# A four-layer decoder step on one core: page numbers batch by batch, weight splits behind ScalarE's copies, two output slots begun with six heads

## The reference, cut to what matters

```python
q, k, v, gate = split(x @ in_w, 4)
# prompt: causal
p = softmax(where(mask, q_c . k_c / 8, -inf)); w = p[:, :, 0] - lam * p[:, :, 1]; o = w @ v
# sample: k_past = cache_k[page_table], v_past = cache_v[page_table]
p = softmax(concat(q . k_past, causal(q . k_new))); w = p[:, :, 0] - lam * p[:, :, 1]
o = w[..., :n_past] @ v_past + w[..., n_past:] @ v
o = rms_norm(o, subln_w) * (1 - lam_init)
mixer = (o * silu(gate)) @ out_w
x = layer_norm(alpha * x + mixer)
```

## Time and profile before

| | |
|---|---|
| median of 3 runs | 1701.72 us |
| lowest, highest | 1694.31, 1703.77 us |
| the profiled execution, its own time | 1699.08 us |
| its span | 1697.4 us |
| mean granted TensorE clock in it | 0.93 |
| busy PE, PEld, DVE, ACT, POOL | 87%, 79%, 63%, 42%, 35% of the span |
| the attention layer in it | from about 205 to 850 us |

### The profile page before, as it was taken

The page is one execution under the profiler, slowest core; times in us unless marked ns, Lnnn a source line. Parts: engine busy times, 40 slices in busy tenths (PEclk is TensorE's granted clock), DMA queues, the critical chain, the costliest instruction groups (busy, mean ns, idle before and its releaser), DMA issues.

```text
span 1697.4 us, 33841 instructions
## 1 busy us (share of the span) xinstructions
PE 1483.8 (87%) x12754; PEld 1346.8 (79%) x12754; DVE 1064.0 (63%) x2293; ACT 716.4 (42%) x1352; POOL 601.9 (35%) x681
## 2 busy tenths in 40 slices
PE   5998977999989897867879999999999789889985
PEld 5887966877777775647779999999999679788885
DVE  4788560445545646556735797779777654668866
ACT  1667231434443433331423454545454332366732
POOL 1545523211112220106414354445435445245441
PEclk7999978999999999988778999999999789899997
DMA  3222205566665656541113234233314222132221
GB/s 114 76 68 78 67 16 162 164 192 194 183 181 183 205 157 199 172 122 50 38 42 88 67 103 113 62 108 104 102 53 127 66 74 87 50 104 66 67 67 66
DMA packets 282539, 179.75 MB, mean 106 GB/s; under 512 B 18906, under 2 KB 280826, under 8 KB 282376
## 3 DMA queue, kind: packets, MB, share of 16 engines
q1 hardware_dynamic: 282376, 177.58, 35.7%
HBM read 160.67 MB, written 16.86 MB: 105 GB/s over the span
## 4 chain that ended last, share of the span: by engine, by line
PE 60%; DVE 21%; issue 7%; ACT 6%; SPq 3%; DMA 2%; POOL 1%; ACTq 0%; DVEq 0%; POOLq 0%
PE proj_lo L1591 10%; PE proj L1591 10%; PE proj_lo L197 6%; PE proj L197 4%; PE proj_lo L868 4%; PE proj L868 3%; PE r L879 2%; DVE conv L476 2%; PE x L963 2%; PE s L1638 2%; SPq L743 2%; DVE rms L1269 2%; PE s L891 1%; DVE h L525 1%; DVE h L530 1%
## 5 line engine op out<-in xcount | busy, mean ns | idle before, releaser
L172 POOL TENSOR_TENSOR w_low<-w_raw,w_high 128x256 fp32r<-128x256 f32 x608 | 537.4, 914 | 1025.7 <-ACT w_high L163 1025.6
L163 ACT ACTIVATE w_high<-w_raw 128x1024 fp32r<-128x1024 f32 x152 | 160.3, 1054 | 178.4 <-PE proj_lo L1591 51.7
L1591 PE MATMUL proj<-xh,w_high 128*128 128x288 f32 x440 | 139.4, 317 | 3.5 <-POOL w_low L172 3.5
L1591 PE MATMUL proj<-xh,w_low 128*128 128x288 f32 x440 | 133.3, 303 | 0.0
L1591 PE MATMUL proj<-xl,w_high 128*128 128x288 f32 x440 | 133.0, 302 | 0.0
L1591 PE MATMUL proj_lo<-xh,w_high 128*128 128x256 f32 x440 | 128.7, 293 | 2.1 <-ACT u L1845 2.1
L1591 PE MATMUL proj_lo<-xl,w_high 128*128 128x256 f32 x440 | 125.5, 285 | 0.0
L1591 PE MATMUL proj_lo<-xh,w_low 128*128 128x256 f32 x440 | 124.5, 283 | 0.0
L1591 PEld LDWEIGHTS proj_lo<-xh,w_high 128*128 128x128 f32 x440 | 84.8, 193 | 13.9 <-issue 11.6
L1591 PEld LDWEIGHTS proj<-xh,w_high 128*128 128x128 f32 x440 | 86.8, 197 | 5.7 <-POOL w_low L172 3.9
L868 PE MATMUL proj<-xh,w_high 128*128 128x288 f32 x248 | 76.8, 310 | 15.9 <-POOL w_low L172 15.9
(11 more groups left out here) (464 smaller groups left out, 4451.8 us busy)
## 6 DMA issues: line engine op xcount, KB each, us to landing
k_pages<-in_cache_k SPq DMA_DIRECT2D x256, 128.0 KB, 2.4
v_pages<-in_cache_v SPq DMA_DIRECT2D x256, 128.0 KB, 2.3
w_raw<-in_c_in_w SPq DMA_DIRECT2D x48, 512.0 KB, 4.0
w_raw<-in_a_in_w SPq DMA_DIRECT2D x32, 512.0 KB, 4.0
w_raw<-in_b_in_w SPq DMA_DIRECT2D x32, 512.0 KB, 4.6
w_raw<-in_a_out_w SPq DMA_DIRECT2D x16, 512.0 KB, 4.1
st<-in_state_ssd_h SPq DMA_DIRECT2D x16, 512.0 KB, 5.1
out_ssd_h_sample<-st SPq DMA_DIRECT2D x16, 512.0 KB, 5.5
```

The costliest lines, as they stand in the source:

```text
L163: act.activation(k.wh[par][:], k.raw[par][:], ACT.Copy).then_inc(k.sem["w_hi"], 1)
L172: step = pool.tensor_tensor(k.wl[par][:, tiles, :], k.raw[par][:, tiles, :], k.wh[par][:, tiles, :], ALU.subtract)
L1591: mm = pe.matmul(out, w[par][:, i, :], x[:, i, cols], start=first and opens and i == 0 and n == 0, stop=last and i == KT - 1 and n == 2, s ...
```

## The change

Three edits to the attention layer.

- SyncE reads the page numbers of one sample (8 numbers, 4 registers) in each of the eight periods of i = 0, behind that period's weight load and ahead of its page loads.
- ScalarE's split of the next slot moves from behind the sample softmax to behind the key copies and the copy of the prompt's weights, ahead of the prompt softmax. Output slot 1 is split in period (4, 7).
- Output slots 0 and 1 are multiplied in parts (`out_part`): slot 0 with heads 0 to 5 in the periods (4, 6), high half, and (4, 7), low half; slot 1's high half with heads 0 to 5 behind the last period; then slot 0 with heads 6 and 7, slot 1's high half with heads 6 and 7, and slot 1's low half with all eight. `out_tensor` then begins with slot 2, `out_scalar` too.

```diff
--- before.py
+++ after.py
@@ -745,9 +745,10 @@
         sp.reg_mov(both, low + high * PAGE)
         return both
 
-    numbers = [page_pair(n) for n in range(0, NB * PAGES, 2)]
-
-    uses = itertools.count()
+    numbers, uses = [], itertools.count()
+
+    def numbers_of(batch):
+        numbers.extend(page_pair(batch * PAGES + g) for g in range(0, PAGES, 2))
 
     def page_of(n, g):
         both, one = numbers[(n * PAGES + g) // 2], sp.alloc_register(f"page_used{next(uses)}")
@@ -795,6 +796,8 @@
                 load_slot(sp, k, s0 + at, at % 2, b_cols(a, at))
             else:
                 load_slot(sp, k, s0 + at, at % 2, a["b_out_w"][0][:, (at - 32) * P:(at - 31) * P])
+        if i == 0:
+            numbers_of(n)
         if i == 0 and n == 1:
             for half in range(2):
                 key_pages(0, 0, half)
@@ -995,6 +998,29 @@
                 t = pe.transpose(out[0:NS, n * P:(n + 1) * P], src[:, SEQ:T], k.ident[:])
         t.then_inc(sem["r_done"], 1)
 
+    def out_part(n, high, heads):
+
+        first, last = heads[0] == 0, heads[-1] == KT - 1
+        if high:
+            cols, out = slice(HALF, T), k.proj[:, n, 0:T - HALF]
+        else:
+            cols, out = slice(0, HALF), k.proj_lo[:, 0:HALF]
+        if first:
+            pe.wait_ge(sem["w_lo"], s0 + 32 + n + 2)
+            if high:
+                pe.wait_ge(sem[f"p_evac{n}"], (u0 + 32) // 2)
+            else:
+                pe.wait_ge(sem["s_evac"], u0 + 32 + n)
+            pe.wait_ge(sem["b_head"], PAIRS - 1)
+        if last:
+            pe.wait_ge(sem["b_head"], PAIRS)
+        for i in heads:
+            for j, (w, x) in enumerate(((k.wh, k.gh), (k.wh, k.gl), (k.wl, k.gh))):
+                mm = pe.matmul(out, w[n][:, i, :], x[:, i, cols], start=i == 0 and j == 0, stop=i == KT - 1 and j == 2)
+        if last and not high:
+            mm.then_inc(sem["pe_slot"], 1)
+
+    early, late = range(2 * PAIRS - 2), range(2 * PAIRS - 2, KT)
     for i, n in b_periods():
         p = Period(i, n)
         if p.scored:
@@ -1009,6 +1035,8 @@
             multiply_new_x(pe, k, s0, u0, 1)
         elif p.slot is not None:
             slot_half(p.slot, True)
+        if (i, n) == (PAIRS, 6):
+            out_part(0, True, early)
         if p.unit:
             past_keys(*p.unit, 1)
         if p.before:
@@ -1021,14 +1049,20 @@
             duo_output(*p.out)
         if p.slot:
             slot_half(p.slot, False)
+        if (i, n) == (PAIRS, 7):
+            out_part(0, False, early)
         if p.scored:
             past_weights(*p.scored)
         if p.before:
             prompt_output(*p.before)
         for slot in p.turned:
             tokens(i, slot)
-    multiply_as_made(pe, k, s0 + 32, u0 + 32, k.gh, k.gl, "b_head", [(PAIRS - 1, range(6)), (PAIRS, (6, 7))])
-    out_tensor(pe, k, s0 + 32, u0 + 32, 1)
+    out_part(1, True, early)
+    for high in (True, False):
+        out_part(0, high, late)
+    out_part(1, True, late)
+    out_part(1, False, range(KT))
+    out_tensor(pe, k, s0 + 32, u0 + 32, 1, first=2)
     ln_tensor(pe, k, 1)
 
 
@@ -1136,20 +1170,22 @@
                     keys_copy(act, k, *p.unit, q, copy)
         if p.scored:
             duo_softmax(*p.scored)
-        if p.slot:
-            at = s0 + p.slot + 1
-            split_high(act, k, at, at // 2, at % 2)
         if p.unit:
             for q in KEYS_ACT:
                 if q >= 2:
                     keys_copy(act, k, *p.unit, q, copy)
         if p.before:
             weights_copy(*p.before)
+        if p.slot:
+            at = s0 + p.slot + 1
+            split_high(act, k, at, at // 2, at % 2)
+        if (i, n) == (PAIRS, 7):
+            split_high(act, k, s0 + 33, (s0 + 33) // 2, 1)
         if p.unit:
             prompt_softmax(*p.unit)
         if p.square:
             squares(*p.square)
-    out_scalar(act, k, s0 + 32, 1)
+    out_scalar(act, k, s0 + 32, 1, ahead=2)
     ln_scalar(act, k, 1)
 
 
@@ -2254,7 +2290,7 @@
     pe.matmul(k.r[:, 0, 0:NS], k.ones_d[:], k.xsum[:, SEQ:T], start=True, stop=True).then_inc(sem["ln_shift"], 1)
 
 
-def out_tensor(pe, k, s, u, layer):
+def out_tensor(pe, k, s, u, layer, first=1):
 
     last, sem = layer == k.last, k.sem
 
@@ -2272,7 +2308,7 @@
                 turn(2 * (n - 4))
         return act
 
-    for n in range(1, KT):
+    for n in range(first, KT):
         multiply_slot(pe, k, s + n, n % 2, u + n, (u + n) // 2, n % 2, k.gh, k.gl, between(n))
         if n == 2:
             ln_shift(pe, k, layer)
```

## The result

The changed kernel takes 1670.41 us, median of four runs (1665.69 to 1674.83); the kernel before takes 1702.74 us beside it (1694.31 to 1703.88). The ratio is 0.9826, 95% interval 0.9806 to 0.9846: 1.5 to 1.9% less, clear of the scatter of the runs, and 1.4 us above the forecast of 1669 us. Run twice more later, it stood at 0.9805 (0.9781 to 0.9829) and 0.9821 (0.9785 to 0.9856); the three medians lie 32.3, 32.8 and 29.7 us under those of the kernel before beside them.

What follows compares the result with a forecast made beforehand. Bounds: the sync queue at the start, ScalarE's order in every second period, VectorE's chain at the end. -16.7 - 11.6 - 3.9 = -32.2 us from 1699.08 gives 1666.9, predicted as 1669 us; eight in ten within 1657 to 1683 us.

Steps and rivals of the forecast that it cites:

- Page numbers: Layer's start: spreading the number loads over eight periods removes 18.2 us and adds a 1.5 us stall, net -16.7 us.
- The removal of 18.2 us: Layer's start: TensorE's 14.49 us idle before slot 2, 2.30 us low clock and 1.37 us second wait go.
- The stall: Second unit: TensorE waits 1.5 us (0 to 5) for key pages issued late by the sync queue's backlog.
- rival C: First units: queue backlog starves them repeatedly, 5 us stall and the same again during value loads; 1678 us, chance 0.10.
- Splits behind the copies: Units: key copy directly follows the sample softmax in 12 periods, 0.97 us earlier each, -11.6 us.
- rival B: Units: the copies' gain passes to the next wait and a third, 3.9 us, remains; 1677 us, chance 0.14.
- D: Units: moved splits make GpSimd's low parts late, so TensorE waits for weights in 26 periods; 1716 us, chance 0.04.
- Output slots: Layer's end: starting output slots early and moving GpSimd's addition sums to -1.3 - 2.4 - 6.8 + 6.6 = -3.9 us.
- +6.6 for -6.8 us: Layer's end: the addition's earlier start removes VectorE's 6.8 us stall but holds the other normalisation 6.6 us (0 to 7.1).
- The clock term of -1.3 us: Stretch at 728-738 us: output-slot matmuls keep TensorE busy, so fuller clock wins 1.3 us (0 to 2.8).
- forecast 2.4 us: After the last head: 18 fewer matmuls stand before output slot 2, saving 2.4 us.
- A: Layer's end: GpSimd's addition moves to where it blocks nothing that matters, the 6.6 us go; 1663 us, chance 0.12.

Runs made afterwards that it cites:

- the run with six additions: Changed kernel with GpSimd's addition of six tiles written as six additions of one tile, same place: 1663.21 us, ratio 0.9782 to the kernel before.
- four batches later: Changed kernel with the page numbers of batches 4 to 7 read behind the second unit's transfers: 1668.77 us, ratio 0.9821 to the kernel before.
- the addition held back: Changed kernel, GpSimd's six-tile addition waiting for the last duo's factors: ratio 0.9793, again 0.9755; with numbers of four batches later 0.9788, of batch 7 later 0.9778.

## Why the prediction was right, point by point

**Page numbers (-16.7 us forecast).** The removal of 18.2 us was right: the keys of the first unit come 18.6, 18.2 and 17.5 us earlier in the three traces. The stall behind it was the step that was mis-sized: forecast 1.5 us, but the first scores come only 13.3, 16.2 and 15.2 us earlier, so it costs 2.0 to 5.2 us, with 1.74 to 3.47 us of waiting (4.09 us in the run with six additions, whose start is the same). The issue time was right to 0.1 us in the first trace (284.31 and 284.92 us in the others); the landing was not. The page's 2.4 us from issue to landing is a median over the whole kernel, and between 283 and 292 us that of the key pages was 3.3 us in the first trace and 3.0 us in the others. A part of the rest is the clock: after the wait of 3.47 us the transposes took 1.97 instead of 1.03 us. Some of rival C was in this, one stall longer than forecast; in place of its second there is none in the first trace and 0.84 and 1.14 us at about 650 us in the others.

**Splits behind the copies (-11.6 us).** Right in what it counted: the splits alone take 11.2 us off the waits at line 900, 0.93 us for each of the 12 periods where the forecast had 0.97 us. (The change as a whole takes 13.0 us off, but 1.8 us of that is output slot 0 in the wait of 3.19 us.) From the first to the last scores more is gained, 12.4, 14.5 and 14.7 us in the three traces and 16.5 us with the part alone; the clock in the units, which was not in the sum, differs there. So rival B, in which the next wait takes it, did not happen, and neither did D: the 0.1 us before line 871 says that no low part came late.

**Output slots (-3.9 us).** The hold went where the forecast put it: the addition starts in the second operation of the normalisation ahead, and the third is held, 7.16 us for 0.43 us. +6.6 for -6.8 us was right: 6.7 and 6.8 us.

The clock term of -1.3 us did not stand up. The forecast put it at 728 to 738 us, ahead of the last scores, so it is read from the end of the wait at line 900 to VectorE's normalisation behind it. That is 17.64 us before (728.15 to 745.79 us) and 16.39 us in the changed kernel (702.11 to 718.50 us), with a granted clock of 0.68 and 1.00 over the first 10 us: 1.25 us, as forecast. But the kernel without output slots needs hardly more, 16.58 us:

```profile
698.34 0.41 PE L903 MATMUL r<-ident,p_prompt 128*128 128x128 f32 x2 [3.19 <-ACT past_k_feat L1059]
```

```profile
714.92 0.75 DVE L1279 SCALAR_TENSOR_TENSOR o_feat<-o_feat,subln,rms 128x512 f32<-128x512 f32 x1
```

The numbers alone need 16.64 us and the splits alone 16.43 us; all three have a clock of 0.83 over those 10 us. So the output slots do come with the fuller clock, but net of their own matmuls it is worth 0.0 to 0.3 us on the path, and the rest of the 1.25 us is that the one traced execution of the kernel before was slower in this place than those three. The stretch from the last scores to the last head misleads here: it falls from 34.28 to 32.65 us with the output slots alone, but only since slot 0's low columns now stand ahead of the last scores and push them back, to 0.71 us before the normalisation in the changed kernel instead of 2.28 us. From the first operation of that normalisation to the last head it is 32.00 us before and 31.93 us with the output slots alone.

What I had not in the sum is that a slow stretch of 1.7 us may or may not fall on the values of the last pair: they took 3.58 to 3.60 us in the three traces of the changed kernel and with the splits alone, and 1.93 us in that of before. Slot 2 came 1.9 us nearer to the last head (9.59 us before, 7.71 us now), forecast 2.4 us; its low part was done 7.2 us behind the last head, as forecast, and just hidden.

**The sum.** -32.2 us forecast, -27.4, -32.2 and -31.7 us at the start of the next layer. In the first trace the stall (3.4 us more than forecast) and the end of the layer (2.2 us more, the slow values) make up the difference, less 0.8 us for the splits. In the other two the stall costs 0.5 and 1.5 us more than forecast and the end of the layer gives 2.4 and 2.2 us less, and the units give 2.9 and 3.1 us more, which was not forecast. So that the total came out within 2 us is luck in part: the queue, the order of ScalarE's work and the moved hold were right, and the errors in sizes, those of the stall and the clock above all, cancelled.

**Rivals.** A did not happen by itself, for the reason given against it, but its 6.6 us can be had: one wait on GpSimd, off the path, takes 6.7 us. (Its 1663 us is 1662.4 us by its own terms, which changes nothing.)

## What to carry to other kernels

When a long operation of GpSimd moves, look at what VectorE does in its new place: here it was held for as long as one instruction of GpSimd lasted, so put the long one behind VectorE's chain, or cut it. Work taken off a path by spreading it over a queue comes back where that queue has the least room; find that place by the issue times, and move only the piece that does not fit. Judge an edit by places near it in several traces, since the span of a single one here moves by 8 us on its own, and by places that the edit itself does not move: the last scores, pushed back by the output slots, showed a gain of 1.6 us that was none.

## What the runs showed of the hardware

The operation that GpSimd's addition held was a TENSOR_SCALAR with one input from SBUF, 7.16 us for 0.43 us, not one with two inputs as I had it in mind. The Trainium skill's page "SBUF — State Buffer", section "Who interferes with whom", names `tensor_scalar` among those that can take the shared ports; the rows agree with it. In the run with six instructions operations with two inputs were held too (0.69 to 1.70 us), and both sides lost, 3.2 us on VectorE and 2.0 us on GpSimd. This is a wait without a semaphore: nothing in the two engines' lists makes that operation wait for the addition.

The low clock did not follow the length of the idle. Behind 8.57 to 8.59 us of idle the values of the last pair took 3.58 to 3.60 us in the three traces of the changed kernel, and 1.93 us with the output slots alone and with four batches later. Behind 3.40 us they took 3.60 us with the splits alone, and 1.93 us before, with the numbers alone and without output slots. Behind 1.84 to 1.86 us they took 3.55 to 3.60 us in the four traces with the addition held back. From 728 to 736 us the granted clock was 0.50, the 1.2 GHz level, in the first trace of the changed kernel and with four batches later alike. It is the way back that differs, in two views of TensorE's stretches:

```profile
736.00:742.00 6.00, 4.75 (x76) 0.60 0.01 3
```

for the changed kernel (length, busy, granted clock, DMA share, GB/s), and with four batches later (busy of TensorE, its weight loads, VectorE, ScalarE and GpSimd, then the clock)

```profile
736.00:742.00 6.00, 4.06 (x79) 2.74 (x79) 0.97 (x5) 1.85 (x3) 0.00 (x0) 0.97 0.01 3
```

What sets the moment of the return is open; it was not tried by itself.
